# The 16 smallest experts in blocks of 64 rows, with two weight passes and a fold, sorted behind the 128-row blocks

## The reference

```python
logits = xt @ router_w + router_b
top_val, top_idx = lax.top_k(logits, 4)
gate = softmax(top_val)
# token/expert pairs sorted by expert, each expert's group padded to MOE_BLOCK = 128 rows
def expert_block(xblk, e):                     # one block of rows, one expert
    hh = xblk @ w1[e] + b1[e]                  # 128 x 1024 @ 1024 x 2048
    glu = minimum(hh[:, :D_FF], 7.0)
    lin = clip(hh[:, D_FF:], -7.0, 7.0)
    act = glu * sigmoid(1.702 * glu) * (lin + 1.0)
    return act @ w2[e] + b2[e]                 # 128 x 1024 @ 1024 x 1024
y = segment_sum(expert_block(...) * row_gate)  # four experts' rows added per token
x_new = x_new + g_f * y
```

## Time and profile before

| | us |
|---|---|
| three timed runs | 2272.94, 2271.85, 2271.79 (median 2271.85) |
| the profiled execution's span (first to last instruction) | 2269.9 |
| so around the span, against the median | 2.0 |
| TensorE busy in the span | 2235.8 (98%) |
| VectorE busy | 1768.0 (78%) |
| ScalarE busy | 1238.6 (55%) |
| GpSimd busy | 429.3 (19%) |
| mixture of experts, from its first matmuls to the end | about 1087 to 2269.9 |

### The profile page before, as it was taken

How to read it: one execution, slowest core, us unless ns; L and a number is a source line. 1 busy time by engine, 2 the same in 40 slices (tenths; PEclk the granted TensorE clock), 3 DMA queues, 4 the chain that set the end, 5 groups by cost and what they waited for, 6 DMA issues and landing times.

```text
span 2269.9 us, 30685 instructions
## 1 busy us (share of the span) xinstructions
PE 2235.8 (98%) x10681; PEld 1828.9 (81%) x10681; DVE 1768.0 (78%) x1652; ACT 1238.6 (55%) x1154; POOL 429.3 (19%) x421
## 2 busy tenths in 40 slices
PE   7999999999999999999999999999999999999998
PEld 3888888888887887888788888888888888888886
DVE  6756655555646766757899999999999999999997
ACT  6322132222225624632777777777777777777774
POOL 3000000000221132102522222222212222223222
PEclk9999999999999999999999999999999999999999
DMA  8322223131321121146899999999999999999995
GB/s 301 121 93 93 98 88 130 56 130 57 105 98 38 38 75 38 57 149 215 310 360 367 374 373 375 386 367 371 381 362 372 370 369 383 370 376 372 385 365 199
DMA packets 135516, 542.98 MB, mean 239 GB/s; under 512 B 16131, under 2 KB 24467, under 8 KB 101390
## 3 DMA queue, kind: packets, MB, share of 16 engines
q1 hardware_dynamic: 123192, 516.30, 60.1%
q0 software_dynamic: 11952, 21.44, 3.9%
q10 hardware_dynamic: 296, 4.21, 0.5%
HBM read 533.79 MB, written 26.38 MB: 247 GB/s over the span
## 4 chain that ended last, share of the span: by engine, by line
PE 95%; DMA 2%; DVE 1%; POOL 1%; ACT 0%; issue 0%; SPq 0%; POOLq 0%; DVEq 0%
PE ps L2272 90%; PE ps L2828 1%; PE ps L2840 1%; PE ps L2619 1%; POOL list_d L865 1%; DMA ar<-h_d,ar 0%; DMA ar<-in_ctx 0%; PE ps L2564 0%; DMA out_x<-ar,cur 0%; DMA raw<-in_w_mod 0%; PE ps L2510 0%; PE ps L2384 0%; DVE nmx L1875 0%; ACT hhi L1026 0%; PE ps L2717 0%
## 5 line engine op out<-in xcount | busy, mean ns | idle before, releaser
L2272 PE MATMUL ps<-whi,yhi 128*128 128x512 f32 x1072 | 346.5, 393 | 0.1
L2272 PE MATMUL ps<-hhi,yhi 128*128 128x512 f32 x1072 | 342.6, 389 | 0.0
L2092 DVE TENSOR_TENSOR hlo<-raw,hhi 128x2048 fp32r<-128x2048 f32 x132 | 302.6, 2294 | 47.3 <-ACT hhi L1333 47.3
L1333 ACT ACTIVATE whi<-raw 128x2048 fp32r<-128x2048 f32 x132 | 253.5, 1921 | 98.9 <-PE ps L2272 98.9
L2092 DVE TENSOR_TENSOR wlo<-raw,whi 128x2048 fp32r<-128x2048 f32 x132 | 298.7, 2282 | 3.4 <-ACT whi L1333 1.9
L1333 ACT ACTIVATE hhi<-raw 128x2048 fp32r<-128x2048 f32 x132 | 253.1, 1918 | 76.5 <-PE ps L2272 76.5
L1450 DVE TENSOR_TENSOR wlo<-raw,whi 128x2048 fp32r<-128x2048 f32 x56 | 128.2, 2289 | 159.5 <-ACT whi L995 159.4
L2272 PEld LDWEIGHTS ps<-whi,yhi 128*128 128x128 f32 x1072 | 201.2, 188 | 53.9 <-issue 12.1
L2272 PEld LDWEIGHTS ps<-hhi,yhi 128*128 128x128 f32 x1072 | 201.2, 188 | 41.7
L2272 PE MATMUL ps<-whi,hhi 128*128 128x512 f32 x592 | 233.3, 394 | 0.0
L2272 PE MATMUL ps<-whi,hlo 128*128 128x512 f32 x592 | 230.8, 390 | 0.0
(11 more groups left out here) (355 smaller groups left out, 4436.6 us busy)
## 6 DMA issues: line engine op xcount, KB each, us to landing
raw<-in_exp_w SPq DMA_DIRECT2D x264, 1024.0 KB, 7.7
ar<-in_exp_w SPq DMA_DIRECT2D x132, 1024.0 KB, 7.6
raw<-in_w_in SPq DMA_DIRECT2D x44, 1024.0 KB, 5.0
raw<-in_w_mod SPq DMA_DIRECT2D x22, 1024.0 KB, 6.4
raw<-in_w_br_ret SPq DMA_DIRECT2D x8, 1024.0 KB, 5.0
ar<-in_x SPq DMA_DIRECT2D x8, 512.0 KB, 7.4
raw<-in_w_br_diff SPq DMA_DIRECT2D x4, 1024.0 KB, 5.1
raw<-in_w_out SPq DMA_DIRECT2D x4, 1024.0 KB, 9.6
```

Source lines behind the costliest of these rows:

```text
L1333: act.activation(e_whi[j % ESPL], e_raw[s], ACT.Copy).then_inc(e_hi, 1)
L2092: V.tensor_tensor(e_wlo[j % ESPL], e_raw[s], e_whi[j % ESPL].bitcast(F32), ALU.subtract).then_inc(e_lo, 1)
L2272: return pe.matmul(out, lhsT, rhs, start=start, stop=stop, skip_group_check=skip)
```

## The change

Blocks 0 to 15 stay 128 rows wide (`WIDE = 16`); blocks 16 to 31 and every extra block have 64 rows. The routing now ranks the experts by their count (experts 0 and 1 are put first whatever their count, since their loads start before the ranking is known), and the block order follows the rank. With the counts above the 16 experts behind the first 16 have 59 rows at most (626 in all), and the expert with 163 rows has one extra block of 35 rows, so there are again 33 blocks: 16 wide, 17 narrow.

In a narrow block the 64 rows' high parts stand in columns 0 to 63 of the stationary operand and their low parts in columns 64 to 127. One matmul with the high weight and one with the low weight then give all products: two passes for three. The results of the low rows stand in partitions 64 to 127 of PSUM and have to be added to those in partitions 0 to 63: ScalarE copies them to SBUF (`lower_up`, `lower_y`), and TensorE adds them with a 64-deep matmul against a shifted identity (`fold_up`, 4 matmuls; `fold_y`, 2 matmuls). The activation and the output scaling then work on 64 partitions, and wait for the fold. On VectorE the order at the block's end is changed: `lo_e(i, 11)` and `x_low` go ahead of the activation, and `lo_e(i+1, 0)` between its two operations. SP reads each block's expert from a table, from block 2 on. The rest of the diff (semaphores that are shared now, the list of rows in 64-row parts) changes no work in the blocks.

```diff
-MAX_BLOCKS = L * TOP_K // P - 1 + N_EXPERTS
-OVER = MAX_BLOCKS - N_EXPERTS
+H = P // 2
+SLOTS_H = L // H
+FULL, REST = divmod(L * TOP_K, (SLOTS_H - 1) * H + 1)
+OVER = FULL * (SLOTS_H - 2) + max(0, (REST - 1) // H - 1)
+MAX_BLOCKS = N_EXPERTS + OVER
 ITEMS = MAX_BLOCKS + 2
+WIDE = N_EXPERTS // 2
+LAST = N_EXPERTS - 1
+NEWS = OVER + 2
+
+
+def narrow(b):
+
+    return b >= WIDE
+
+
+def nth(b):
+
+    return b - WIDE
...
@@ -735,12 +754,11 @@
             load_w1(0, 0, RSLOTS - 1)
             for j in range(ERAW, FIRST):
                 load_w1(0, 0, j)
-            with sp.Fori(1, N_EXPERTS) as i:
-                for j in range(FIRST):
-                    load_w1(i, i, j)
-                for k in range(MOE_N - FIRST):
...
             def extra(i):
                 e = sp.value_load(items_i[0:1, bass.ds(i + ITEMS, 1)], min_val=0, max_val=N_EXPERTS - 1)
@@ -750,6 +768,8 @@
                 for k in range(MOE_N - FIRST):
                     load_w2(e0, i, FIRST + k, k)
 
+            with sp.Fori(2, N_EXPERTS) as i:
+                extra(i)
             end = sp.value_load(count_i[0:1, 1:2], min_val=N_EXPERTS - 1, max_val=MAX_BLOCKS - 1)
 
...
+            def lower_up(i):
+
+                act.wait_ge(e_used, chunk(i, FIRST - 1) + 1)
+                for c in range(2):
+                    act.activation(low_banks[:, 2 * c:2 * c + 2, :], ps[H:P, 2 + 2 * c:4 + 2 * c, :],
+                                   ACT.Copy).then_inc(up_low, 1)
+
+            def lower_y(i):
+
+                act.wait_ge(e_used, chunk(i + 1, MOE_N - 1) + 1)
+                act.activation(low_banks[:, 0:2, :], ps[H:P, 6:8, :], ACT.Copy).then_inc(y_low, 1)
+
+            def item(i, half_b, half_a, half, half_n, n=None):
+
                 for j in range(AHEAD, ESPL):
                     hi_e(i, j)
-                if isinstance(i, int):
-                    act.sem_inc(y_out, 1)
-                act_high(i - 1)
+                if half_b:
+                    lower_y(i - 2)
+                act_high(i - 1, half_a)
                 for j in range(ESPL, MOE_N - 1):
                     hi_e(i, j)
-                glu(i)
-                hi_e(i, MOE_N - 1)
-                x_high(i + 1)
+                if half:
+                    lower_up(i)
+                    hi_e(i, MOE_N - 1)
+                    x_high(i + 1, half_n)
+                    glu_half(n)
+                else:
+                    glu(i)
+                    hi_e(i, MOE_N - 1)
+                    x_high(i + 1, half_n)
                 for j in range(AHEAD):
                     hi_e(i + 1, j)
+
...
             dve.wait_ge(route_step, 2)
-            V.tensor_scalar(small[0:96, 0:1], ps[0:96, 3, 0:1], cst[0:96, C_THR:C_THR + 1], None,
-                            ALU.is_gt).then_inc(flag_ready, 1)
+            tl.did(V.tensor_copy(count, ps[0:E, 3, 0:1]))
+            tl.did(V.tensor_scalar(key, ps[0:E, 3, 0:1], float(E), key_add, ALU.mult, ALU.add))
+            tl.did(V.scalar_tensor_tensor(out=row_key, in0=ps[0:E, 3, E:2 * E], scalar=float(E), in1=row_add,
+                                          op0=ALU.mult, op1=ALU.add))
+            tl.wait()
+            tl.did(V.tensor_scalar(full[:, 1:SLOTS_H], iota[0:E, 1:SLOTS_H], float(H), count, ALU.mult, ALU.is_lt))
+            tl.did(V.tensor_scalar(above, row_key, key, None, ALU.is_gt))
+            tl.wait()
+            tl.did(V.tensor_reduce(n_full, full[:, 1:SLOTS_H], AX.X, ALU.add))
+            tl.did(V.tensor_reduce(rank, above, AX.X, ALU.add))
+            tl.wait()
+            tl.did(V.tensor_scalar(is_wide, rank, WIDE - 0.5, None, ALU.is_lt))
+            tl.did(V.tensor_scalar(at_rank, iota[0:E], rank, None, ALU.is_equal))
+            tl.wait()
+            V.tensor_scalar(n_more, n_full, is_wide, 0.0, ALU.subtract, ALU.max).then_inc(flag_ready, 1)
...
+            def activate_half(i, n, between):
+
+                dve.wait_ge(up_full, n * 2 + 2)
+                V.tensor_scalar(ac[0:H], psf[0:H, 4 * COL:6 * COL], 1.0 - LIMIT, 1.0 + LIMIT, ALU.max,
+                                ALU.min).then_inc(moe_step, 1)
+                between()
+                dve.wait_ge(glu_done, i + 1)
+                dve.wait_ge(moe_step, i + 1)
+                V.scalar_tensor_tensor(out=ac[0:H], in0=gs[0:H], scalar=GLU_TOP, in1=ac[0:H], op0=ALU.min,
+                                       op1=ALU.mult).then_inc(act_done, 1)
+
...
+            def give_half(i, n):
+
+                dve.wait_ge(cur_ready, i + 1)
+                dve.wait_ge(y_full, n)
+                V.scalar_tensor_tensor(out=F(A_Y, D)[0:H], in0=psf[0:H, 6 * COL:8 * COL],
+                                       scalar=cur[0:H, 1:2].bitcast(F32), in1=F(A_GFB, D)[0:H], op0=ALU.mult,
+                                       op1=ALU.mult).then_inc(y_out, 1)
+
+            def item(i, half_b, half_a, half, half_n, n=None, n_b=None):
+
                 for j in range(AHEAD, ESPL):
                     lo_e(i, j)
-                act_low(i - 1)
-                if not isinstance(i, int):
+                act_low(i - 1, half_a)
+                if half_b:
+                    give_half(i - 2, n_b)
+                elif not isinstance(i, int) or i > 1:
                     give_y(i - 2, chunk(i - 1, MOE_N - 1))
                 for j in range(ESPL, MOE_N - 1):
                     lo_e(i, j)
-                activate(i, lambda: lo_e(i, MOE_N - 1))
-                x_low(i + 1)
-                for j in range(AHEAD):
-                    lo_e(i + 1, j)
+                if half:
+                    lo_e(i, MOE_N - 1)
+                    x_low(i + 1, half_n)
+                    activate_half(i, n, lambda: lo_e(i + 1, 0))
+                    lo_e(i + 1, 1)
+                else:
+                    activate(i, lambda: lo_e(i, MOE_N - 1))
+                    x_low(i + 1, half_n)
+                    for j in range(AHEAD):
+                        lo_e(i + 1, j)
+
...
+            item_at(1)
+            item_at(2)
+            with dve.Fori(3, WIDE - 1) as i:
+                item(i, False, False, False, False)
+            for i in range(WIDE - 1, WIDE + 2):
+                item_at(i)
+            with dve.Fori(WIDE + 2, N_EXPERTS) as i:
+                item(i, True, True, True, True, i - WIDE, i - 1)
...
+            def turn_x(half=False):
+                m = H if half else P
                 for q in range(2):
                     for c in range(4):
                         k = 4 * q + c
-                        last = pe.transpose(ps[:, q, c * P:(c + 1) * P], F(A_XG, D)[:, k * P:(k + 1) * P], ident)
+                        last = pe.transpose(ps[:, q, c * m:(c + 1) * m], F(A_XG, D)[0:m, k * P:(k + 1) * P],
+                                            ident[0:m, 0:m])
                     last.then_inc(xt_turned, 1)
 
...
-            def up(i, between=None):
+            def up(i, half=False, between=None):
...
                         mm(o, xthi[:, kk, :], wh, late and kk == 0, False)
-                        mm(o, xthi[:, kk, :], wl, False, False)
-                        last = mm(o, xtlo[:, kk, :], wh, False, kk == KC - 1)
+                        last = mm(o, xthi[:, kk, :], wl, False, half and kk == KC - 1)
+                        if not half:
+                            last = mm(o, xtlo[:, kk, :], wh, False, kk == KC - 1)
                     last.then_inc(e_used, 1)
                     if between:
                         between(kk)
 
-            def down(i, at_i, chunks):
+            def down_chunk(j, kk, o, c, half):
+
+                q = kk % 2
+                cols = slice(q * D + c * COL, q * D + (c + 1) * COL)
+                wh, wl = e_whi[j % ESPL][:, cols], e_wlo[j % ESPL][:, cols]
+                mm(o, acthi[:, kk, :], wh, kk == 0, False)
+                last = mm(o, acthi[:, kk, :], wl, False, half and kk == KC - 1)
+                if not half:
+                    last = mm(o, actlo[:, kk, :], wh, False, kk == KC - 1)
+                return last
+
+            def down(i, at_i, half, chunks):
+
                 if 0 in chunks:
                     pe.wait_ge(act_lo, i * 2 + 2)
                     pe.wait_ge(y_out, i + 1)
@@ -2880,33 +3071,61 @@
                     j = FIRST + k
                     pe.wait_ge(e_lo, chunk(at_i, j) + 1)
                     for q in range(2):
-                        kk = 2 * k + q
                         for c in range(2):
-                            o = ps[:, 6 + c, :]
-                            cols = slice(q * D + c * COL, q * D + (c + 1) * COL)
-                            wh, wl = e_whi[j % ESPL][:, cols], e_wlo[j % ESPL][:, cols]
-                            mm(o, acthi[:, kk, :], wh, kk == 0, False)
-                            mm(o, acthi[:, kk, :], wl, False, False)
-                            last = mm(o, actlo[:, kk, :], wh, False, kk == KC - 1)
+                            last = down_chunk(j, 2 * k + q, ps[:, 6 + c, :], c, half)
```

(46 more changed lines are left out.)

369 lines of the change are left out of this document (221 added, 148 removed).

## The result

| | before | after |
|---|---|---|
| median of the runs shown together | 2271.82 us (2271.29 to 2272.94) | 2336.59 us (2334.66 to 2337.40) |
| ratio, 95% interval | | 1.0284 [1.0269, 1.0299] |
| span of the profiled execution | 2269.9 us | 2334.9 us |

The time lies 80 us above the upper end of the range, and on the other side of no change. It answers to none of the rivals.

What follows compares the result with a forecast made beforehand. TensorE was taken to set the pace, with the DMA engines second. From 2269.9 us: routing +2, wide blocks +1, loads -36.2, end lag -8.2, last fold +1, a span of 2229.5; median forecast 2231.5 us, range 2206 to 2257.

Steps and rivals of the forecast that it cites:

- What is added: Extra costs: routing +2 us, wide blocks +1, kernel's end +1; SP's table reads 0, GpSimd's scatter and gather 0.
- ScalarE's block: ScalarE's work per narrow block: 28.3 us, not the pace; handovers have 0.5 to 1 us of slack.
- the sum: All terms against the profiled execution's 2269.9 us: -40.4 us, a span of 2229.5.
- Rival 3: TensorE's clock falls at waits in narrow blocks, half the matmuls at 1.2 GHz: 37 us a block, 2304 us; chance 0.06.
- Routing: Some 12 small VectorE operations added before the first block: +2 us (0 to 3).
- The wide blocks: Full 128-row blocks need more DMA; some six in a row run 0.5 us over the pace: +1 us (0 to 5).
- VectorE's work: VectorE's operations in one narrow block: 31.3 us, less than the DMA engines need.
- The DMA engines' pace: Weight loads and row moves set the narrow block's pace: 33.15 us (32.4 to 34.2) for 35.30; -36.2 us in all.
- The lag at the end: From the last load's landing to the last matmul, 16.6 us before: shrinks by 8.2 us (4 to 10.2), won once.
- Rival 1: The DMA share stays 0.985 in narrow blocks: pace 34.2 us, 2249 us; chance 0.19.
- rival 2: DMA engines give more than expected, so VectorE bounds narrow blocks at 31.3 us: 2200 us; chance 0.10.
- Rival 4: A handover (fold, `lower_up`, activation) late by about 1.5 us in each block: 2255 to 2272 us; chance 0.08.

Runs made afterwards that it cites:

- e7_fold: The changed kernel with `fold_y` ahead of the bias matmuls, so ahead of the wait for the selector; 2246.55 us, ratio 0.9893.
- e6_pause: The changed kernel, but in narrow blocks VectorE's low parts from the sixth on each wait for the end of the one before; 2261.59 us, ratio 0.9952.
- e14_low_first: e7_fold with ScalarE's `lower_y` copy ahead of the fourth high part instead of behind it; 2256.62 us, ratio 0.9933.
- e15_low_first_less: e14_low_first with each block's four down-weight loads halved from the 17th block on (10 MB a block); 2250.07 us, ratio 0.9905.
- e18_low_first_pause1: e14_low_first with one pause a block: VectorE's second low part behind `give_half` waits for the end of the one before; 2234.15 us, ratio 0.9838.
- p5_probe: Small kernel without the layer's work, varying the shape of the operation ahead of ten VectorE subtractions; scatter 22.0 to 22.4 us behind 64x1024, 2.6 behind the five larger-or-128-partition shapes.
- head_then_gap: Small-kernel case: VectorE's first of ten subtractions waits for the end of the 64x1024 operation ahead; scatter 2.6 to 2.7 us, against 21.5 to 22.4 without a gap.
- e2_sel: The changed kernel, but in narrow blocks GpSimd makes the next block's selector ahead of `take_rows`; 2323.84 us, ratio 1.0244.
- e11_busy7: The changed kernel with 14 filling matmuls on TensorE ahead of `up()` in each narrow block, at its wait for the selector; 2338.16 us, ratio 1.0294.

## Why the prediction was wrong

**The step that failed** is the last sentence of *What is added*: "GpSimd's scatter and gather wait for others before, and move fewer rows now: 0". It counted bytes and waits, and left out that the operations around the scatter on another engine change shape and lose their gaps. The scatter's instruction took 18.07 us for 2.79 and landed after 24.6 us for 10.7, and the selector queued behind it. The narrow block's pace became 39.06 us for 33.15. SP issues its last load at 2295.5 us (below) for a predicted 2202, and these 93.5 us are most of the 105.4 by which the span exceeds the sum's 2229.5.

```profile
2292.91 2.58 SPq L735 DMA_DIRECT2D ar<-in_exp_w  x2
```

**A second step**, in *ScalarE's block*: "`fold_y` one us before `give_half`. The slack is small, 0.5 to 1 us, but it is nowhere negative." `fold_y` stands behind the selector's wait, and I followed the low parts but not that wait. It is what turned a long scatter into a loop. No single run takes the loop away and leaves every hold, since in e7_fold (2246.55 us) the hold goes too from the second narrow block on. But e6_pause has `fold_y` in its old place and no hold but the first, at a pace of 34.00, and e14_low_first has it ahead and 7 more held scatters at a pace of 33.93, with steps of some 37 us where they are held. Both together make 39.06.

**A smaller term that the sum lacked** is the clock. The sum has TensorE at full clock; it fell in every narrow block and cost 1.9 us of the loop. Rival 3 named the place, TensorE's wait for the activation, but put half of the matmuls at the lower level, 12 us more a block.

**What held.** Routing: +1.85 us for +2. The wide blocks: 35.30 us apart, nothing lost for +1. TensorE is no bound in the narrow blocks. VectorE's work, 31.3 us: e15_low_first_less runs steps of 31.2. The DMA engines' pace, 33.15 (32.4 to 34.2): 32.53 in e18_low_first_pause1, at a share of 1.02 for the 1.015 taken, so a block took 33.2 us of engine time for 33.65. With the hold away that kernel's 2234.15 us is 2.7 from the 2231.5 that was forecast, which is partly luck, as the next term shows.

**A term that was mis-sized even there.** The lag at the end should have shrunk by 8.2 us. From SP's last issue to the start of the last matmul it was 24.1 us before (2235.2 and 2259.3), 28.0 after (2295.5, 2323.5) and 26.9 in e18_low_first_pause1 (2195.3, 2222.2). Its VectorE and TensorE at the end:

```profile
2213.37 4.48 DVE L2183 TENSOR_TENSOR hlo<-ar,hhi 128x2048 fp32r<-128x2048 f32 x2
```

```profile
2222.24 0.50 PE L2436 MATMUL ps<-hlo,hhi 64*128 64x512 f32 x1 [0.68 <-ACT hlo L1529]
```

The last two low parts stand behind `give_half` in VectorE's queue, so a load that lands earlier is not used earlier. So the lag did not shrink by 8.2 us but grew by 2.8. The pace, 0.62 us better than taken over some 16 blocks, 9.9 us, made up for most of it.

**The rivals.** Rival 1 (DMA full, 2249) and rival 2 (VectorE, 2200) had their resources right: in e18_low_first_pause1 the DMA share is 1.02, and late in it VectorE sets the pace. Rival 3 named the clock: the granted clock was 0.84, as a result of waits that have another cause. Rival 4, a bubble of 1.5 us in a handover, had the right kind; the handover to GpSimd was not on its list, and it was 5.9 us a block.

**Still open.** What in VectorE or GpSimd makes a train with a 64x1024 operation hold when the other shapes tried do not (no other length on 64 partitions but 2048, and no number of partitions below 64, was tried), and why one PSUM piece does not end a hold when the pair of `x_low` does. Not tried: `give_half` and the activation on all 128 partitions, which would need no pause if p5_probe carries over.

## What to carry to other kernels

Taking work off the fullest engine does not come for free if a third one depends on how the second runs: before a change that makes VectorE run back to back, or halves the partitions of its operations, look at how long GpSimd's DMA instructions take now and which gap or which shape of operation lets them in. Walk every wait of an instruction that is placed behind another one, the selector's as well as the data's, and close the loop on paper: what is the round from this step to itself, and what if one of its links grows by 15 us? One added wait on the fullest engine brought 22 us (e14_low_first to e18_low_first_pause1). And where an experiment fills a wait to keep a clock up, see in its trace that the filling ended in time, before an unchanged time is read as "the clock costs nothing".

## What the runs showed of the hardware

- GpSimd's indirect DMA is held by a gapless train of two-SBUF operations on VectorE once a 64x1024 operation stands in that train, up to the end of those operations: 22.4 us under ten subtractions, 18.07 in the kernel. The Trainium skill ("SBUF — State Buffer", Who interferes with whom) says that a VectorE instruction with two SBUF inputs contends with a GpSimd instruction that reads SBUF, and that the loser waits until the other has finished; the 2.6 to 2.8 us under other trains agree with that (the rest of one subtraction and 1.3 us: in `head_then_gap` it ended at 109.66 us, the scatter at 110.94). The trace goes against it in two points, and the measurement decides: the loser waited not for one instruction but for up to ten, and the page's sentence that `tensor_tensor` was not seen stalling a DMA does not hold for this indirect one.
- Small operations of GpSimd that read SBUF are held as well: `take_rows` took 3.24 us for 0.18 with VectorE out of the way, and a copy of 64x2 took 18.42 us for 0.19 in e2_sel.
- TensorE's granted clock fell to 0.50, the lower level of 1.2 GHz, once in each narrow block. It fell at 1874.4 us, while TensorE waited for the activation (idle from 1871.96 to 1874.50), ahead of the wait for the selector (1875.58 to 1881.22), and came back at 1884.6. With the second wait filled (e11_busy7) it fell at the same place and came back 3.4 us later; the mean rose to 0.92, not to 1.00. Three stretches of the changed kernel (columns as in the earlier trace rows):

```profile
1873.00:1874.30 1.30, 0.00 (x0) 0.00 (x0) 1.30 (x3) 1.30 (x2) 0.00 (x0) 1.00 1.04 372
1874.50:1881.00 6.50, 1.08 (x8) 0.90 (x8) 6.50 (x4) 2.37 (x4) 3.33 (x2) 0.50 1.01 388
1884.70:1890.00 5.30, 5.30 (x23) 3.84 (x22) 1.89 (x2) 3.72 (x2) 0.00 (x0) 1.00 0.74 248
```
